# A long convolution whose spectral products are made across two passes, and whose last inverse transform is summed in two rounds

## The reference

```python
def hyena_filters(L, w1, b1, w2, b2, w3, b3, freq):
...
    h = (hid @ _f32(w3) + _f32(b3)).reshape(L, HY_ORDER, 2, HY_WIDTH)
...
    h = h * jnp.exp(-t * jnp.abs(deltas))[:, None, None, :]
    fwd, bwd = h[:, :, 0], h[:, :, 1]
    kern = jnp.concatenate([fwd, jnp.zeros((1, HY_ORDER, HY_WIDTH), jnp.float32), bwd[:0:-1]], axis=0)
    kern = kern / jnp.sum(jnp.abs(kern), axis=0, keepdims=True)
    return jnp.fft.rfft(kern, axis=0)

def long_conv(u, k_f, skip):
    y = jnp.fft.irfft(jnp.fft.rfft(uf, n=2 * L, axis=1) * k_f, n=2 * L, axis=1)[:, :L]
    return (y + uf * _f32(skip)).astype(u.dtype)
...
    for o in range(HY_ORDER):
        z = parts[o + 1] * long_conv(z, k_f[:, o], skip[o])
```

## Time and profile before

| | us |
|---|---|
| median of 3 runs | 4913.47 (4912.9 to 4920.15) |
| the profiled execution, its own time | 4910.12 |
| its span | 4908.1 |
| PE busy in the span | 4173.6 (85%) |
| DVE busy | 1898.4 (39%) |
| the long convolution, first matmul to end of last | 578.1 |

### The profile page before, as it was taken

One profiled execution on the slowest core, in us unless ns is written; L12 is line 12 of the kernel. 1 busy time (PEld: TensorE's weight loads), 2 busy tenths in 40 slices (PEclk: granted clock), 3 DMA queues, 4 the chain that ended last, 5 costly groups with the idle time before them and its releaser, 6 DMA issues. The chain is left out here.

```text
span 4908.1 us, 59293 instructions
## 1 busy us (share of the span) xinstructions
PE 4173.6 (85%) x20947; PEld 2139.3 (44%) x20947; DVE 1898.4 (39%) x2965; ACT 1097.4 (22%) x1816; POOL 258.2 (5%) x366
## 2 busy tenths in 40 slices
PE   3699699998999998999679997786999599949995
PEld 0355355555444445777534444442333244413331
DVE  1233345443322113898734936532111333321112
ACT  0122255443110012222111135310000234100000
POOL 0000000000000000110100000000000200000001
PEclk7799899999999998999889999997999799969998
DMA  7322221112365511111161112135865511266666
GB/s 258 117 68 63 60 49 38 37 36 84 139 218 210 200 64 56 42 39 52 43 211 35 43 54 102 53 104 232 321 264 214 187 31 49 100 265 228 251 235 261
DMA packets 260939, 627.18 MB, mean 128 GB/s; under 512 B 73549, under 2 KB 153501, under 8 KB 240969
## 3 DMA queue, kind: packets, MB, share of 16 engines
q1 hardware_dynamic: 221906, 508.13, 29.3%
q0 software_dynamic: 19424, 94.01, 5.1%
q10 hardware_dynamic: 19480, 23.31, 1.3%
HBM read 1298.29 MB, written 113.53 MB: 288 GB/s over the span
## 5 line engine op out<-in xcount | busy, mean ns | idle before, releaser
L1645 PE MATMUL hyp_acc<-hy_hT,hyp_early_weights 128*128 128x512 f32 x768 | 335.9, 596 | 0.0
L3423 PE MATMUL blocks_h<-moe_w,blocks_xT 128*32 128x512 f32 x2560 | 291.1, 607 | 42.3 <-issue 42.3
L3423 PE MATMUL blocks_h<-od_hT,blocks_xT 128*32 128x512 f32 x1280 | 290.9, 608 | 25.7 <-DMA moe_w1b<-in_ex_w 20.6
L3444 PE MATMUL blocks_acc<-moe_w,blocks_hidT 128*32 128x512 f32 x2560 | 284.5, 596 | 11.2 <-DMA moe_w<-in_ex_w 9.9
L3423 PE MATMUL blocks_h<-moe_w1b,blocks_xT 128*32 128x512 f32 x1280 | 290.8, 608 | 0.0
L970 PE MATMUL att_scores<-att_kT,att_qT 64*128 64x512 f32 (+3 forms) x768 | 252.2, 549 | 22.7 <-DMA att_v<-scratch_V 22.7
L700 PE MATMUL lat_acc<-lat_w_in,lat_hT 128*128 128x512 f32 (+1 forms) x640 | 244.6, 538 | 2.2 <-DMA lat_w_in<-in_attn_w_in 2.2
L2209 PE MATMUL evp_acc<-ev_hT,evp_early_weights 128*128 128x512 f32 x512 | 224.6, 600 | 7.6 <-DVE evp_qkT L2350 5.6
L906 DVE TENSOR_REDUCE att_nmax<-att_scores 128x1 f32<-128x1280 f32 x128 | 190.2, 1486 | 102.2 <-PE att_scores L970 102.2
L994 PE MATMUL att_turn<-ident,att_probs 128*128 128x128 f32 x1280 | 192.5, 281 | 42.3 <-DVE att_o L936 22.5
L1645 PEld LDWEIGHTS hyp_acc<-hy_hT,hyp_early_weights 128*128 128x128 f32 x768 | 145.1, 191 | 174.3 <-issue 174.2
(11 more groups left out here) (520 smaller groups left out, 6067.5 us busy)
## 6 DMA issues: line engine op xcount, KB each, us to landing
moe_w<-in_ex_w SPq DMA_DIRECT2D x320, 2048.0 KB
od_hT<-in_ex_w SPq DMA_DIRECT2D x80, 2048.0 KB
moe_w1b<-in_ex_w SPq DMA_DIRECT2D x80, 2048.0 KB
hyp_m_weights<-in_mod_w POOLq DMA_DIRECT2D x6, 8192.0 KB, 24.2
mod_weights<-in_ada_w SPq DMA_DIRECT2D x6, 4096.0 KB, 22.7
scratch_y_rows<-blocks_x ACTq DMA_DIRECT2D x40, 512.0 KB, 8.9
hyp_early_weights<-in_hy_w_in SPq DMA_DIRECT2D x8, 2048.0 KB
scratch_parts<-hyp_uT SPq DMA_DIRECT2D x24, 512.0 KB, 3.7
```

The costliest lines, as they stand in the source:

```text
L1645: mm = nc.tensor.matmul(acc[:, m % 2, half * NC:(half + 1) * NC], weights[:, ws, kt, c:c + P], hT[:, kt, half * NC:(half + 1) * NC], start ...
L3423: mm = nc.tensor.matmul(out[mine, :], xT[:, kt, mine], w[l][:, kt, :], start=(kt == 0), stop=(kt == KT - 1))
L3444: mm = nc.tensor.matmul(acc[mine, c, :], hidT[:, kt, mine], w2[l][:, kt, c * NC:(c + 1) * NC], start=(kt == 0), stop=(kt == FT - 1))
```

## The change

The change is in the long convolution alone. The product of one half of the frequencies becomes a function `spectra(i, ft, parts)` of four parts: enter (the butterfly of `xu`, into a new buffer `work`), multiply, combine, and leave (the turn back into z). The first half of pass i + 1 does its first three parts in the body of pass i, and its last one in the body of pass i + 1.

To have `xu` in time, the u transform of pass i + 1 moves into the body of pass i, behind the filter transform and the first four filter tiles of pass i + 2; ahead of it PE waits until DVE has emptied the four banks (`tiles_gone`), since the transform uses them. The last four filter tiles come behind it. ACT's copies move likewise. The two `k_butterfly` of pass i + 1 move ahead of all scaling of pass i. In the prologue the u transform of pass 0 stands between the two halves of the filter tiles of pass 1, and DVE does three parts of the first half of product 0 behind the eighth tile of pass 1 and ahead of its totals.

In the last pass the product is written into `filt`, not into `z`, so it need not wait for the inverse of pass 6, and parts of it stand between the scalings of pass 6. The last inverse (`last_inverse`) is summed in two rounds: for the first half of the frequencies all four phases, then for the second half; phases 2 and 3 go to `x_bank` 2 and 3, so that four banks are open at once.

The skip weights are loaded pass by pass (1 KB each), and `ktmp` shares `tmp`.

```diff
-        skip, skip_in = sb("skip", [1, PASSES * CCH]), sem("skip_in")
+        skip = sb("skip", [1, CCH])
...
-        tmp, ktmp = sb("tmp", [P, PH, 2, CCH]), sb("ktmp", [P, 2, 2, CCH])
+        tmp, work = sb("tmp", [P, PH, 2, CCH]), sb("work", [P, PH, 2, CCH])
+        ktmp = tmp[:, 0:2, :, :]
...
+        z_last = filt[:, :, :, :].rearrange("p (m r) v c -> p m r v c", r=PH)
+        def product_of(i):
+            return z_last if isinstance(i, int) and i == PASSES - 1 else z
+        def y_place(i, r):
+            return x_bank[r] if r >= 2 and isinstance(i, int) and i == PASSES - 1 else y_bank[r % 2]
 
...
+                def u_transform(j):
+                    pe.wait_ge(u_in, signals(j * 16 + 16))
+                    transform(u_parts, lambda ft: u_copied(j, ft) - 1, u_made)
+
+                def tiles_gone(j):
+                    for b in range(PH):
+                        pe.wait_ge(filt_ready, signals(j * NF + (b + 1)))
...
-                    filters(1, range(NF))
+                    filters(1, range(PH))
+                    tiles_gone(1)
+                    u_transform(0)
+                    filters(1, range(PH, NF))
                     norm(1)
 
+                def last_inverse(i):
+                    for ft in range(MT):
+                        pe.wait_ge(z_made, signals(i * MT + (ft + 1)))
+                        for r in range(PH):
+                            if ft == 0:
+                                if r < 2:
+                                    pe.wait_ge(y_scaled[r], signals(i * (PH // 2)))
+                                else:
+                                    pe.wait_ge(x_copied[r], signals(i * COPIES + COPIES))
+                            for t in range(MT):
+                                for cs in range(2):
+                                    mm = nc.tensor.matmul(y_place(i, r)[:, t, :], inv[:, ft, r, cs, t * P:(t + 1) * P],
+                                                          product_of(i)[:, ft, r, cs, :],
+                                                          start=(ft == 0 and t == 0 and cs == 0),
+                                                          stop=(ft == MT - 1 and t == MT - 1 and cs == 1))
+                            if ft == MT - 1:
+                                mm.then_inc(y_made, 1)
                 def body(i, more, ahead):
+                    if not more:
+                        return last_inverse(i)
                     if more:
                         pe.wait_ge(filt_ready, signals(i * NF + 2 * NF))
-                    pe.wait_ge(u_in, signals(i * 16 + 16))
-                    transform(u_parts, lambda ft: u_copied(i, ft) - 1, u_made)
-                    if more:
                         k_transform(i + 1)
                     if ahead:
                         filters(i + 2, range(PH))
+                        tiles_gone(i + 2)
+                    if more:
+                        u_transform(i + 1)
+                    if ahead:
+                        filters(i + 2, range(PH, NF))
                     pe.wait_ge(z_made, signals(i * MT + MT))
                     for r in range(PH):
-                        if ahead and r == 1:
-                            filters(i + 2, range(PH, NF))
                         if ahead and r == PH - 1:
                             norm(i + 2)
                         pe.wait_ge(y_scaled[r % 2], signals(i * (PH // 2) + r // 2))
                         for t in range(MT):
                             last = gather(y_bank[r % 2][:, t, :], [
-                                (inv[:, ft, r, cs, t * P:(t + 1) * P], z[:, ft, r, cs, :])
+                                (inv[:, ft, r, cs, t * P:(t + 1) * P], product_of(i)[:, ft, r, cs, :])
                                 for ft in range(MT) for cs in range(2)])
                         last.then_inc(y_made, 1)
...
+                        if made is u_made and not (isinstance(n, int) and n == 0):
+                            act.wait_ge(xu_read, signals(n * MT + (ft + 1 - MT)))
...
-                    act.wait_ge(z_made, signals(i * MT))
-                    copies(i, u_made, xu)
                     if more:
                         k_copies(i + 1)
                     if ahead:
                         decays(i + 2)
+                    if more:
+                        copies(i + 1, u_made, xu)
+                    if ahead:
                         sizes(i + 2)
...
+                def spectra(i, ft, parts):
+                    links = Chain(dve, u_steps, i * (MT * U_STEPS) + ft * U_STEPS)
+                    x, k, w = xu[:, ft, :, :, :], vk[:, ft, :, :, :], work[:, :, :, :]
+                    def enter():
+                        dve.wait_ge(x_copied[PH - 1], signals(u_copied(i, ft)))
+                        dve.wait_ge(vk_ready, signals(i * MT + MT))
+                        dve.wait_ge(z_made, signals(i * MT + ft))
+                        tt(tmp[:, 0:2, :, :], x[:, 0:2, :, :], x[:, 2:4, :, :], ALU.add)
+                        tt(tmp[:, 2:4, :, :], x[:, 0:2, :, :], x[:, 2:4, :, :], ALU.subtract).then_inc(xu_read, 1)
+                        dve.wait_ge(xu_read, signals(i * MT + (ft + 1)))
+                        links.link(turn(nc.vector, tmp[:, 0, :, :], tmp[:, 1, :, :], tmp[:, 2, :, :], tmp[:, 3, :, :], w, 1))
+                    def multiply():
+                        links.n = 1
+                        links.link(tt(tmp[:, :, :, :], w, k, ALU.mult))
+                        tt(w[:, :, 0, :], w[:, :, 0, :], k[:, :, 1, :], ALU.mult)
+                        links.link(tt(w[:, :, 1, :], w[:, :, 1, :], k[:, :, 0, :], ALU.mult))
+                    def combine():
+                        links.n = 3
+                        links.link(tt(tmp[:, :, 0, :], tmp[:, :, 0, :], tmp[:, :, 1, :], ALU.subtract))
+                        links.link(tt(tmp[:, :, 1, :], w[:, :, 0, :], w[:, :, 1, :], ALU.add))
+                        tt(w[:, 0:2, :, :], tmp[:, 0:2, :, :], tmp[:, 2:4, :, :], ALU.add)
+                        links.link(tt(w[:, 2:4, :, :], tmp[:, 0:2, :, :], tmp[:, 2:4, :, :], ALU.subtract))
+                    def leave():
+                        if product_of(i) is z:
+                            dve.wait_ge(y_made, signals(i * PH))
+                        turn(nc.vector, w[:, 0, :, :], w[:, 1, :, :], w[:, 2, :, :], w[:, 3, :, :],
+                             product_of(i)[:, ft, :, :, :], 3).then_inc(z_made, 1)
+                    for part in parts:
+                        (enter, multiply, combine, leave)[part]()
...
-                    filters(1, range(NF))
+                    filters(1, range(PH))
+                    filters(1, range(PH, NF))
+                    spectra(0, 0, range(3))
...
+                    last = isinstance(i, int) and i == PASSES - 1
+                    if not last:
+                        spectra(i, 0, [3])
+                        spectra(i, 1, range(4))
                     if ahead:
                         filters(i + 2, range(PH))
+                    if more:
+                        for ft in range(MT):
+                            k_butterfly(i + 1, ft)
+                        spectra(i + 1, 0, range(2))
+                    if ahead:
                         filters(i + 2, range(PH, NF))
                     dve.wait_ge(rn_made, signals(i + 1))
                     for r in range(PH):
+                        if more and r == 1:
+                            spectra(i + 1, 0, [2])
+                        if more and not ahead:
+                            if r == 2:
+                                spectra(i + 1, 0, [3])
+                            if r == 3:
+                                spectra(i + 1, 1, [0])
                         if ahead and 0 < r <= 2:
                             totals(i + 2, range((r - 1) * PH // 2, r * PH // 2))
-                        if more and r >= PH - MT:
-                            k_butterfly(i + 1, r - (PH - MT))
                         if ahead and r == PH - 1:
                             tap(i + 2)
                         dve.wait_ge(y_made, signals(i * PH + (r + 1)))
                         dve.wait_ge(conv_done, signals(i * PH + max(r - 1, 0)))
-                        tt(y[:, r % 2, :, :], y_bank[r % 2][:, :, :], rnorm[:, :].unsqueeze(1).to_broadcast([P, MT, CCH]),
+                        tt(y[:, r % 2, :, :], y_place(i, r)[:, :, :], rnorm[:, :].unsqueeze(1).to_broadcast([P, MT, CCH]),
                            ALU.mult).then_inc(y_scaled[r % 2], 1)
+                    if more and not ahead:
+                        spectra(i + 1, 1, range(1, 4))
```

More of the change, by code:

```diff
@@ L1833, in load_u, with load_skip @@
                     sp.dma_start(tiled(u), tokens(i)).then_inc(u_in, 16)
-                sp.dma_start(skip[:, :], skips).then_inc(skip_in, 16)
+                def load_skip(j):
+                    sp.wait_ge(tapped, signals(j))
+                    sp.dma_start(skip[:, :], skips[:, bass.ds(j * CCH, CCH)]).then_inc(skip_in, 16)
```

(44 more changed lines are left out.)

5 lines of the change are left out of this document (3 added, 2 removed).

## The result

The changed kernel takes **4936.52 us** (median of 5 runs, 4934.4 to 4941.0), the kernel before 4914.08 in the same comparison (4912.9 to 4920.15). The ratio is 1.0046, with a 95% interval of 1.0031 to 1.0060: slower by 0.46%. The forecast was 4921.5, its range ended at 4936. The profiled execution has a span of 4934.5 us, 26.4 more than before, of which 21.2 lie in this stage.

The account below looks back on a forecast made before the run. PE (60.8 us) and DVE (58.9) both nearly fill a 65.44 us body, so their waits on each other count. 17.6 + 11.8 - 21.0 = +8.4, taken as +8 on 4913.5: 4921.5 us, range 4906 to 4936.

Parts of the forecast that it names:

- Prologue, +17.6: Before the second filter transform: u transform waits 4.6 us, DVE's spectrum parts delay the totals; start at 1974.0, not 1956.4.
- Bodies, +11.8: Six loop bodies of 67.4 us against 65.44, +1.96 each; the wait for z goes and the norm is late next.
- adds nothing if the clock holds: Loop body, TensorE's 2.3 us gap before the u transform: no cost if the clock stays full.
- at 2.3 us it is nearer to the first: Loop body: the gap before the u transform was judged closer to 1.99 us, clock held, than to 2.81, clock fallen.
- the row at 1.99 us: Earlier TensorE timeline: a gap of 1.99 us left 96 records at 41.44 us, full clock.
- the 2.81 us that had not held: Earlier TensorE timeline: after a gap of 2.81 us, 8 records took 6.17 us for 3.6.
- The slower rival: Clock falls in the gap before each u transform: 2.0 us six times, +20, 4933 us; chance 0.2.
- The norm was priced: Loop body, after a TensorE gap of about 4 us: norm at 3.45 + 2.0 us for the fallen clock.
- The skip loads: Eight loads of 1 KB in SP's queue, nothing due ahead of the filter transform's end, 20.7 us: put at nothing.
- Tail, -21.0: From the eighth filter transform: 72.8 us to the last product, then 6.9 + 2.0; 81.7 us against 102.7.
- The row's 1.1 us: Loop body: each of two DVE pieces meeting a POOL product takes 1.1 us longer, as read from DVE's earlier timeline.
- the lock as a whole product paid at each collision: Loop body: by the shared-port lock two collisions would cost 2.5 us, not 2.2, the stage 2 us more; not adopted.

Follow-up runs that it names:

- pro_early: The changed kernel with enter and multiply of the first spectra ahead of the second half's filter tiles in the prologue; 4927.22 us, ratio 1.0021.
- fill_u: The changed kernel with five extra unused matmuls on TensorE ahead of each wait for the four banks before the u transform; 4924.36 us, ratio 1.0014.
- combine_late: The changed kernel with DVE's combine part in the loop moved behind the totals; 4896.13 us, ratio 0.9957.

## Why the prediction was wrong

**Prologue, +17.6.** Right: 16.7 in the changed kernel. The u transform waited 4.9 us (4.6 worked out), the norm 18.9 (some 19), and pro_early shows for 7.9 us of that wait that its cause was the named one. A prologue in this order took from 98.8 to 101.9 us in seven profiles, so that 16.7 falls within 1 us of the forecast is in part luck.

**Bodies, +11.8.** Wrong: +25.0. Taken by its own pieces over the five later bodies (mean 70.25 us against 67.4): from the filter transform to the u transform 26.9 us (26.4 from the y beside it); from there to the norm 34.1 (20.9 + 10.9 = 31.8); from the norm to the next filter transform 9.2 (9.2). So all but 0.5 us of the excess is in one piece, and in it in the u transform: records of 16.35 us in the mean, where 13.98 stood before. The failed step is the sentence that the gap before it "adds nothing if the clock holds", and the choice behind it: "at 2.3 us it is nearer to the first", the row at 1.99 us. The gap was 2.57 us, nearer to the 2.81 us that had not held. With the 0.5 us ahead of the transform that makes 5 x 2.85 = 14.2 us, less 1.0 for the first body: the 13.2 by which the bodies exceed the forecast. fill_u, which only fills the gap, holds the clock and gives bodies of 68.2.

The slower rival said this, with its place and its mark (u transform at 15.8), at a chance of 0.2 and 4933 us. In the stage it was near: it had 2.0 us in six bodies, 12; the fall came in five, at 1.4 to 2.9 us, 2.3 in the mean, so nearly 12 too, and its sum of +20 stands against the stage's +21.2. Of the 3.5 us from 4933 to 4936.5 most lies outside the stage and in rounding. The norm was priced right: its record takes 5.84 us in the mean and 3.62 at full clock, 2.2 more where 2.0 was forecast, after the wait of 4.0 that was forecast too. The skip loads, which were put at nothing, show no price: the instruction that reads them (`lc_extra`) is held up by the norm alone, 43.4 us in all eight passes.

**Tail, -21.0.** Right: -20.5. The last product was made 72.7 us after the eighth filter transform (72.8 worked out), and the rounds left 9.5 us behind it (8.9 in the forecast).

**Collisions with POOL.** The row's 1.1 us was somewhat high: 0.95 on the combination (2.17 against 1.22) and 0.73 on a total (1.42 against 0.69). The rows read as the turn-taking by whole instructions that the Trainium skill states (SBUF — State Buffer, section "SBUF: two separate sides"): POOL's product, issued at 2093.08 inside DVE's L2125, lasts 2.17 us and not 1.27, and DVE's L2126 starts at 2094.17 and ends 1.1 us after it. The prediction read the lock as a whole product paid at each collision, 2.5 us in a body. What DVE pays is what is left of POOL's product when its own instruction comes. L2126 came 1.1 us ahead of the end of POOL's product and took 0.95 longer; the total at 2101.70 came 0.9 us ahead of the end of the next one (2102.57) and took 0.73 longer. The body paid 1.7.

**Left over.** The time rose by 22.4 us and the stage by 21.2. The profiled span rose by 26.4: the stage starts 2.05 us later in the changed kernel's profile than before, and what follows it is 3.1 us longer. Both lie outside the change. The stage starts at 1870.7 to 1876.0 us in the profiles, with the same code ahead of it, so the start is scatter.

## What to carry to other kernels

Where a reordering makes TensorE wait for another engine at a new place, price the wait and the matmuls behind it, even when the wait is 2.5 us: here a gap of 2.57 us took 2.3 us more from the transform behind it, in the mean, and a gap of 4.0 us 2.2 more from a short norm. Between two rows that bracket a gap, put both outcomes into the sum with near equal chance rather than choosing the nearer one. And when splitting a stage's vector work moves it to new places, look at once for what else stands in VectorE's queue ahead of a small result that the other engine needs (here the totals of the norm): moving one combination of 5 us behind them was worth 40 us, more than the 22.4 that the whole change cost.

## What the runs showed of the hardware

- A gap of 2.57 us before a transform lowered the clock 20 times of 20, one of 1.4 us 4 times of 17, one of 1.71 us, behind fillers, never in 5: the length of the gap alone does not predict it. In combine_late the five gaps of 2.03 us gave 15.76, 14.07, 15.76, 14.07 and 15.76 us in turn.
- Five matmuls whose results are not used (ten records, 2.32 us of TensorE) saved 2.3 us in the transform behind them, and two of them (four records, 1.03 us) did as well. The granted clock in that transform went from 0.82 or 0.90 to 1.00 in fill_u.
- The transform behind a fall takes 15.76 us after 1.4 or 2.0 us of gap and 15.5 to 17.1 after 2.57: against 14.1 at full clock the fall costs from 1.4 to 3.0 us, not a fixed sum.
- Where a VectorE instruction with two inputs in SBUF came while a GpSimd product ran, it took longer by 0.95 and 0.73 us, with 1.1 and 0.9 us of the product left; the product is 1.27 us long when free.
